# Mixture of experts: a step takes two half tiles of 64 rows in two lanes of TensorE's columns, weights not split

## The reference

```
gl = xf @ w_group + b_group;  g = argmax(gl)                  # top 1 of 4 groups
el = xf @ w_erouter + b_erouter;  el_g = el of group g
tv, ti = top_k(el_g, 2);  wi = softmax(tv)                    # top 2 of 4 experts
gates = softmax(gl)[g] * wi
a = silu(x @ w_gate) * (x @ w_up)                             # 1024 -> 256 each
y = sum over the two experts of (a * gate) @ w_down           # 256 -> 1024
```

## Time and profile before

| | |
|---|---|
| profiled execution | 1260.89 us |
| its span, first to last instruction | 1259.1 us |
| mean granted TensorE clock | 0.967 |
| TensorE busy | 1142.3 us (91%) |
| VectorE busy | 699.0 us (56%) |
| ScalarE busy | 597.0 us (47%) |
| GpSimd busy | 141.0 us (11%) |
| the chain that ended last, largest shares | DMA scratch_x 8%, gate_up 8%, down 5% |

### The profile page before, as it was taken

The page is one execution under the profiler, slowest core; times in us unless marked ns, Lnnn a source line. Parts: engine busy times, 40 slices in busy tenths (PEclk is TensorE's granted clock), DMA queues, the critical chain, the costliest instruction groups (busy, mean ns, idle before and its releaser), DMA issues. The chain is left out here.

```text
span 1259.1 us, 23319 instructions
## 1 busy us (share of the span) xinstructions
PE 1142.3 (91%) x7695; PEld 821.1 (65%) x7695; DVE 699.0 (56%) x1048; ACT 597.0 (47%) x1030; POOL 141.0 (11%) x172
## 2 busy tenths in 40 slices
PE   7999999999789889959889999998499999999992
PEld 6877888888445556635555667876367666667771
DVE  4322112220167767658798996543566766666664
ACT  5530122201176767637466664222165655556654
POOL 1100000000011111100000000000123222333311
PEclk9999999999899999979999999999599999999997
DMA  6642243317599999999999955433679999875476
GB/s 209 217 133 77 83 146 126 100 42 250 197 366 381 381 365 332 380 369 381 382 376 383 318 210 174 161 125 117 265 276 363 377 378 292 235 173 115 100 217 193
DMA packets 155392, 307.43 MB, mean 244 GB/s; under 512 B 22311, under 2 KB 49354, under 8 KB 151178
## 3 DMA queue, kind: packets, MB, share of 16 engines
q1 hardware_dynamic: 145018, 272.38, 60.1%
q0 software_dynamic: 9216, 33.56, 11.3%
q10 hardware_dynamic: 1040, 0.00, 0.0%
HBM read 308.31 MB, written 54.72 MB: 288 GB/s over the span
## 5 line engine op out<-in xcount | busy, mean ns | idle before, releaser
L327 PE MATMUL proj_ps<-w_in_split,x_T_hi 128*128 128x512 f32 x608 | 194.5, 395 | 2.7 <-DVE w_in_split L369 2.7
L2516 DVE TENSOR_TENSOR w_gate_up_split<-w_gate_up,w_gate_up_split 128x2048 fp32r<-128x2048 f32 x62 | 139.3, 2288 | 84.5 <-ACT w_gate_up_split L2574 84.5
L2467 PE MATMUL gate_up_ps<-w_gate_up_split,slot_rows_T 128*128 128x512 f32 x744 | 177.7, 394 | 3.3 <-DVE slot_rows_T L2524 3.3
L2467 PEld LDWEIGHTS gate_up_ps<-w_gate_up_split,slot_rows_T 128*128 128x128 f32 x744 | 137.4, 188 | 32.2 <-DVE slot_rows_T L2524 4.5
L327 PEld LDWEIGHTS proj_ps<-w_in_split,x_T_hi 128*128 128x128 f32 x608 | 115.0, 189 | 27.7 <-DVE x_T_lo L364 2.5
L455 ACT ACTIVATE proj_rows<-proj_ps,sum_squares 128x512 f32<-128x512 f32 x38 | 26.2, 689 | 211.5 <-PE proj_ps L327 199.7
L327 PE MATMUL proj_ps<-w_in_split,x_T_lo 128*128 128x512 f32 x304 | 119.1, 392 | 0.0
L2574 ACT ACTIVATE w_gate_up_split<-w_gate_up 128x2048 fp32r x62 | 115.3, 1913 | 4.7 <-DMA w_gate_up<-in_w_up 3.1
L2489 PE MATMUL expert_out_ps<-w_down,expert_act_T 128*128 x256 | 115.3, 593 | 0.2 <-issue 0.2
L1736 PE MATMUL mix_out_ps<-w_out_split,oT_split 128*128 128x512 f32 x420 | 101.2, 396 | 0.3 <-DVE w_out_split L1875 0.3
L1142 PE MATMUL turns_and_scores_ps<-head_kT,head_qT 64*128 64x512 f32 (+3 forms) x384 | 81.8, 537 | 15.7 <-issue 10.7
(11 more groups left out here) (255 smaller groups left out, 1733.1 us busy)
## 6 DMA issues: line engine op xcount, KB each, us to landing
w_gate_up<-in_w_gate SPq DMA_DIRECT2D x34, 1024.0 KB, 8.4
w_gate_up<-in_w_up SPq DMA_DIRECT2D x34, 1024.0 KB, 10.2
w_down<-in_w_down SPq DMA_DIRECT2D x34, 1024.0 KB, 12.2
pages<-in_cache_v_d SPq DMA_DIRECT2D x128, 256.0 KB, 5.8
pages<-in_cache_kT_s SPq DMA_DIRECT2D x128, 256.0 KB, 5.2
pages<-in_cache_v_s SPq DMA_DIRECT2D x128, 256.0 KB, 5.1
pages<-in_cache_kT_d SPq DMA_DIRECT2D x100, 256.0 KB, 5.9
w_in_now<-in_w_in SPq DMA_DIRECT2D x48, 256.0 KB, 3.1
```

The source lines that it names most:

```text
L327: last = pe.matmul(pj_ps[:, n % PJ_BANKS, :], h[:, k, at], w[g % 2][:, k, :], start=(k == 0 and m == 0), stop=(k == KC - 1 and m == 2))
L2467: last = pe.matmul(gu_ps[:, u, :], xT[:, u, a, k, :], gu_split[:, u, b, k, :], start=(k == 0 and m == 0), stop=(k == KC - 1 and m == 2))
L2516: dve.tensor_tensor(gu_split[:, u, 1, at, :].rearrange("p k (c n) -> p k c n", c=2), raw[:, at, :, :], gu_split[:, u, 0, at, :].bitcast(F3 ...
```

## The change

- `MOE_TILES` is 25: the slots are now in half tiles of 64 rows (at most 49). A step takes one half tile in lane a, from the first expert up, and one in lane b, from the last expert down. Lane a is columns 0 to 63 of TensorE and partitions 0 to 63 of the results, lane b the rest.
- gate and up are joined by the host into one `w_gu` of 512 columns; one DMA of 2 MB loads both. Lane a has 4 places for weights. Lane b has 2, and its weights are copied from there, half by ScalarE and half by VectorE (`take_gu`, `take_dn`), into a fixed place from which TensorE reads.
- Nothing is split: gate_up is 8 x 2 plain fp32 matmuls of 64 columns, down 4 x 2. The rows are kept in one piece.
- A step makes two scatter-adds of 64 rows, one after the other.
- `route` works out step, lane, and the experts of both lanes.

```
-MOE_TILES = (TOP_K * (SEQ + N_SAMPLE) + N_EXPERTS * (P - 1)) // P
+HALF_TILES = TOP_K * (SEQ + N_SAMPLE) // LANE + N_EXPERTS - 1
+MOE_TILES = (HALF_TILES + 1) // 2
...
+                n_halves = ends[:, E - 1:E]
+                link(dve.tensor_tensor(mirror[:, :], wide(n_halves, [P, PAIRS]), part[:, 0, :], ALU.subtract))
+                link(dve.scalar_tensor_tensor(at_step[:, 0, :], mirror[:, :], -1.0, part[:, 0, :], ALU.add, ALU.min))
+                link(dve.tensor_tensor(lane[:, :], part[:, 0, :], at_step[:, 0, :], ALU.is_gt))
+                link(dve.scalar_tensor_tensor(at_step[:, 1, :], lane[:, :], float(LANE), part[:, 1, :], ALU.mult, ALU.add))
...
 (SyncE)
+                def load_a(tile):
+                    e, load, at = wanted_load(0, tile)
+                    gu_done.reached(sp, tile - A_PLACES, 1)
+                    sp.dma_start(gu_a at place, t.w_gu[e], cond=load).then_inc(gu_a_loaded[tile % A_PLACES], 16)
+                    y_done.reached(sp, tile - A_PLACES, 1)
+                    sp.dma_start(dn_a at place, t.w_down[e], cond=load).then_inc(dn_a_loaded[tile % A_PLACES], 16)
+                def load_b(tile):
+                    e, load, at = wanted_load(1, tile)
+                    for half in range(2):
+                        gu_b_kept[half].reached(sp, tile - B_PLACES)
+                    sp.dma_start(gu_b at place, t.w_gu[e], cond=load).then_inc(gu_b_loaded[tile % B_PLACES], 16)
+                    for half in range(2):
+                        dn_b_kept[half].reached(sp, tile - B_PLACES)
+                    sp.dma_start(dn_b at place, t.w_down[e], cond=load).then_inc(dn_b_loaded[tile % B_PLACES], 16)
+                load_a(0)
                 for tile in range(MOE_TILES):
+                    load_a(tile + 1)
+                    load_b(tile)
...
 (GpSimd, add_rows)
+                    for n, rows_of in enumerate(lanes):
+                        if tile or n:
+                            pool.wait_ge(t.added, 32 * tile + 16 * n)
+                        pool.indirect_dma_start(t.x1[:, :],
+                                                bass.IndirectOffsetOnAxis(ap=t.slot_out[0:LANE, n, tile:tile + 1], axis=0),
+                                                y[rows_of, tile % 2, :], None, compute_op=ALU.add).then_inc(t.added, 16)
...
 (TensorE, gate_up)
+                        pe.matmul(gu_ps[lanes[0], u, :], xT[:, u, k, lanes[0]],
+                                  t.gu_a[:, bass.ds(at, 1), k, :].rearrange("p a n -> p (a n)"),
+                                  start=(k == 0), stop=(k == KC - 1))
+                        last = pe.matmul(gu_ps[lanes[1], u, :], xT[:, u, k, lanes[1]], gu_b[:, k, :],
+                                         start=(k == 0), stop=(k == KC - 1))
...
 (VectorE; ScalarE has the other halves, with gu_done.reached(act, tile - 1, 0))
-                def split_gu(tile):
-                def split_rows(tile):
+                def take_gu(tile):
+                    dve.wait_ge(gu_b_loaded[tile % B_PLACES], 16 * (tile // B_PLACES) + 16)
+                    gu_done.reached(dve, tile - 1, 1)
+                    dve.tensor_copy(gu_b[:, 4:KC, :], t.gu_b[at place, 4:KC, :]).then_inc(gu_b_kept[1].sem, 1)
                 for tile in range(MOE_TILES):
                     if tile + 1 < MOE_TILES:
-                        split_gu(tile + 1)
+                        take_gu(tile + 1)
                     multiply(tile)
                     if tile + 1 < MOE_TILES:
-                        split_rows(tile + 1)
+                        keep_rows(tile + 1)
                     if tile:
                         keep_y(tile - 1)
+                    take_dn(tile)
```

More of the change, by code:

```diff
@@ L2216, in _ @@
-                dve.wait_ge(placed, 1)
+                link(dve.tensor_scalar(n_steps_i[:, :], ends[0:1, E - 1:E], 1.0, None, ALU.add))
+                link(dve.tensor_scalar(n_steps_i[:, :], n_steps_i[:, :], 1, None, ALU.logical_shift_right))
+                link(dve.tensor_copy(n_steps[:, :], n_steps_i[:, :]))
+                link(dve.tensor_scalar(t.adds_wanted[:, :], n_steps[:, :], 32.0, None, ALU.mult))
+                link(dve.tensor_scalar(live[:, :], t.column[0:1, 0:MOE_TILES], n_steps[:, 0:1], None, ALU.is_lt))
@@ L2259, in _ @@
                 pe.wait_ge(step, t.n_te)
-                pe.transpose(te_ps[0:1, 0:P], te[:, :], t.ident[:, :]).then_inc(te_turned, 1)
+                for n in range(2):
+                    pe.transpose(te_ps[0:1, n * P:(n + 1) * P], te[:, n:n + 1], t.ident[:, :]).then_inc(te_turned, 1)
                 pe.wait_ge(lanes_kept, 1)
                 pe.matmul(tok_ps[:, 0:COL_TILE], lanes[:, :], t.sums_of_parts[:, :], start=True, stop=True)\
+                  .then_inc(placed, 1)
+                pe.matmul(tok_ps[0:LANE, TILE_COLS:2 * TILE_COLS], lanes[:, LANE:P], t.sums_of_parts[:, :], start=True, stop=True)\
                   .then_inc(placed, 1)
@@ L2404, in _ @@
+                for lane in range(2):
+                    sp.wait_ge(t.first_loaded[lane], 32)
+                load_a(0)
+                for tile in range(MOE_TILES):
+                    load_a(tile + 1)
+                    load_b(tile)
+                wanted = sp.value_load(t.adds_wanted[0:1, 0:1], min_val=32, max_val=32 * MOE_TILES)
                 sp.wait_ge(t.added, wanted)
@@ L2479, in down @@
                 def down(tile, halves=(0, 1)):
-                    u, at = tile % 2, place(pe, tile)
+                    u, at = tile % 2, place(pe, 0, tile)
                     aT_kept.reached(pe, tile)
-                    pe.wait_ge(dn_loaded[tile % W_PLACES], 16 * (tile // W_PLACES) + 16)
-                    if tile < W_AHEAD:
-                        pe.wait_ge(t.w_ahead[tile], 48)
+                    pe.wait_ge(dn_a_loaded[tile % A_PLACES], 16 * (tile // A_PLACES) + 16)
+                    for half in range(2):
+                        dn_b_kept[half].reached(pe, tile)
                     for c in halves:
```

343 lines of the change are left out of this document (179 added, 164 removed).

## The result

The kernel after takes 1301.76 us (median of 4 runs, 1301.65 to 1303.03), the one before 1262.73 in the same measurement: ratio 1.0307, 95% interval 1.0292 to 1.0322. The change makes it slower by 39 us; the forecast was 1256 with a range of 1238 to 1300. The profiled execution has a span of 1299.5 us, 40.4 more than before.

A forecast was written before the change was run, and what follows sets the result against it. The scatter-adds were taken to bound the changed kernel: first add at 931.5, chain 316 us plus 4 of waits, TensorE's end 1230.8, tail 24.0, span 1254.8, plus 1.8 gives 1256.6, say 1256; range 1238 to 1300.

The forecast's parts named there:

- the chain of adds: Expert stage: 50 scatter-adds, each waiting for the one before, 316 us plus 4 of waiting for TensorE; decides the end.
- the price of a loaded add: A 64-row scatter-add beside the weight stream: 8.2 us where 128 rows took 10.8; quiet 5.0 where it was 7.0.
- the start: Start of the expert stage: the removed wait and the added routing and copies cancel, second gate_up at 919.5.
- the tail: From the last scaling to the end: 24.0 us of norms and stores as before, the last adds beside it.
- lane b's stalls: Turning the activation late at five steps, as lane b's weights land late: 16 us, bounds 0 and double.
- A mostly fixed price: Rival on the scatter-adds: 64 rows keep 6.2 us quiet and 10.0 loaded, time 1305; dear adds' chance 0.27.
- an estimate of 6.4 and 10.2 us: Scatter-adds of 64 rows, quiet and loaded, by the skill page: chain 380 us, time 1311; chance within dear adds' 0.27.
- the later of 1214.5 and 1230.8: TensorE's end in the expert stage: 1214.5 by its own work with late weights, 1230.8 by the scatter-adds, which decides.
- TensorE's step: Expert loop: 11.5 us a step with both lanes side by side, changes between full and half array given nothing.
- ScalarE and VectorE hidden: Weight copies in the expert loop: each engine at some 5 to 6 us a step, under TensorE's 11.5.

The follow-up runs named there:

- x8: The kernel before with each tile's add of 128 rows issued as two of 64 rows, nothing else changed: 113 us slower.
- x3: The kernel after with one add of 128 rows a step, lane b's half to a second region and left out of the output: 1285.4 us.
- x5: The kernel after with lane b's gate_up load queued earlier, no first-step skipped loads, one add a step (lane b's sums left out): 1240.3 us.
- x2: The kernel after without issuing the first step's four loads, which are skipped anyway: gained 10 us.
- x12: The kernel after without the last 8 of its 50 adds, those of the 4 steps without tokens: 1278.4 us.
- x7: The kernel after with lane b's gate_up load earlier, no first-step skipped loads, one add a step, lane b's sums added in the last norm: 1250.9 us.
- x9: The kernel before with plain fp32 gate_up, no split, in one lane of 128 rows, 32 tiles as before: 1298.7 us.

## Why the prediction was wrong

**Wrong sign. That the chain of adds sets the end held; the price of a loaded add, the start, the tail and lane b's stalls did not.** The prediction had slower at 325 us of chain or more; it was 347.7. The forecast's chain in its own terms, beside what was measured: first add 931.5, it was 941.41 (9.9 late). Chain 320, it was 343.2 from the first issue to the last plus 4.5 for the landing (27.7 more). End 3.3 us behind the last landing (1254.8 - 1251.5), it was 1299.5 - 1289.1 = 10.4 (7.1 more). Together 44.7, all of what lies between the spans 1254.8 and 1299.5. By step:

- **The loaded add, the term that decided: mis-sized.** "Halving the data part alone ... I take 5.0 and 8.2". Loaded it was 10.1 beside the weights. Base, halving and what was left out failed in about equal parts. The 10.8 halved is the shortest of six loaded spacings, whose mean is 11.5 (0.7 us); 2.6 were to be saved, and x8 saves 2.0 with the packets as before (0.6 us); the last 0.6 lie between x8 and the kernel after, where packets are longer and the loads come in another order. Quiet was nearly right: of the 30 waited-for spacings under 7.5 us, 27 have a mean of 5.2 (the other three are 6.2 to 7.3). By the prediction's own rule, 153 us of loaded time and the rest quiet, 10.1 makes 15.1 loaded adds where 8.2 made 18.7, and the chain 337 instead of 320: 17 of the 27.7 us. The quiet adds at 5.2 are 7 more, and the last 3 to 4 are not split.
- **The rivals on the add's price.** A mostly fixed price gave 1305 with 6.2 and 10.0. Its loaded price was right and its quiet one 1.0 too dear, so its chain came out at 373 instead of 347.7; that its time is near is luck, since it kept the prediction's start and tail, which were too early. By the Trainium skill (DMA: Bandwidth & Descriptors, Anatomy of one DMA), as used in the prediction, an estimate of 6.4 and 10.2 us was due: the loaded adds agree within 0.4, the quiet ones contradict it by 1.2. The agreement is partly luck: its saving of 0.6 is below the 2.0 of x8, and its base of 10.8 below 11.5.
- **Lane b's late weights: five stalls, as named, but 27.3 us of idle time where 16 were foretold.** The step that failed is "SP reaches load_b(t) only after load_a(t+1)", which was given no time. From the issue of lane a's w_down to that of lane b's gate_up SP takes 2.2 to 2.9 us (976.19 to 978.76 is one), 13.2 us over the five loads, more than the 11.3 that were missing. The landing was right in sum: 3 x 13.0 + 2 x 10.2 = 59 us foretold, 58 measured from issue to copy. That was luck, as the 10.2 of the earlier trace rows is of the loads ahead and not of the loop. What the sum left out as well is the clock: the five full steps behind the stalls take 14.0 to 14.7 us instead of 12.0, 11.6 more, since TensorE's granted clock is at 1.2 GHz behind the gap and records last 0.84 instead of 0.42 for the first 4.4 us. Together 39 us, above the bound of "double", 32; x3 shows 339.9 - 304.7 = 35 when the adds are out of the way.
- **Two bounds, not one and a rest.** I let the later of 1214.5 and 1230.8 decide. In the stage, x5 has 304.7; with late weights alone it is 339.9, with the adds alone 344.6, with both 348.1. They hardly add; each hides the other: taking one away shows 3.5 to 8.2 us of stage, taking both 43. The copies of weights and the kept outputs stand in the same queues of ScalarE and VectorE, so the two waits touch too.
- **The start: "I let both cancel" failed.** 8.6 us late instead (second gate_up 928.06 against 919.48). Most of it is SP's queue, where skipped loads stand ahead of lane b's first: 7.2 us of idle time went with them in x2. I had counted loads that move data, and not SP's way to those that don't. It is the same missing time as in the late weights.
- **The tail: "as before" failed.** The last scaled output waits for dead adds (8.36 us), and four more adds stand behind it, slowed by the final loads (8.1 us for the one of 1276.51). I had named these adds and then laid them beside the norm without asking when they end. x12 takes 15 us off the tail.
- **TensorE's step: pairing right (0.43 us a pair of records), changes of tiling not free.** Foretold 11.5, it is 12.0. The Trainium skill (TensorEngine Tiling (Array Packing), Key Properties) had said that such a change drains TensorE; the trace agrees, with 0.15 us each. The row I set against it had no idle entry, but the cost sits inside the records. Where TensorE sets the stage, as in x5 and x7, it is 24 x 0.6 = 14 us, an estimate; what it is worth in the kernel after no run shows.
- **ScalarE and VectorE hidden**: right as work (both idle most of the step), wrong as queues, which is how the late copies reached TensorE.

What stays open is why any add costs some 4.5 us more beside the weights than in quiet, whether it has 64 rows (10.1 and 5.2) or 128 (11.5 and 7.0). Packet length is at most a part of it; nothing here shows the rest.

## What to carry to other kernels

Splitting a serial chain of read-modify-write DMAs is priced under the load it will run in, not in quiet: half the rows saved 26% of an add in quiet (7.0 to 5.2) and some 17% beside a weight stream (11.5 to 9.5, x8). Take the base of such a price as the mean of several rows; the one row taken here was the cheapest of six. A median time of a DMA may be that of a few issues outside the loop in question: ask for a window. Where two bounds end within a few per cent, an experiment that removes one shows only their difference; remove both before judging either, as 3, 10 and 16 us alone became 61 together (51 with lane b's sums added, x7). Count the instructions that do nothing, skipped loads and dead adds: here they were 10 us at one end and 15 or more at the other.

## What the runs showed of the hardware

- A change between the full array and half tiles on TensorE costs about 0.15 us, shown as a first record of 0.57 instead of 0.42; a pair of fp32 records of 512 columns on the two column halves takes 0.43 us, as long as one record on the full array (x9).
- SP needs some 3 us from one pair of conditional loads to the next, also when nothing is moved (907.04, 910.31, 913.03); an issue itself was 0.08 to 0.43 us.
- Behind each of five gaps of 2.6 to 6.9 us on TensorE its granted clock fell to 1.2 GHz for a while, and the step took 2.0 to 2.7 us longer.
- A scatter-add of 64 rows, by the spacing of chained adds: a mean of 5.2 us in quiet, 9.1 to 9.5 beside a stream of weights in 8 KB packets, 9.3 to 10.1 with 16 KB ones; one of 128 rows: 7.0, and 11.5 to 11.9.
